# Expert weights in DRAM laid out partition by partition: one contiguous run a partition for each load

## The chip, the cores and the metric

The kernel runs on one core of one Trainium2 chip. The metric is the device time of one execution in microseconds. The work is split over the engines of the core: TensorE (PE, with its weight loads shown apart as PEld), VectorE (DVE), ScalarE (ACT), GpSimd (POOL), and SyncE (SP), which here issues nearly all transfers. Sixteen DMA engines move data between DRAM and the on-chip buffer of 128 partitions.

## The reference

The reference is a network of two blocks on 1024 tokens of width 1024, all in float32. The first block has dilated attention, a convolution and attention over a memory, then a convolutional feed-forward layer. The second has differential attention, a gated linear scan, neighbourhood attention, and then the mixture of experts that this change touches:

```python
def hier_moe(h, w_rg, b_rg, w_re, b_re, w_up, w_down):
    # each token picks a group, and 2 of the 8 experts in it (32 experts in all)
    # tokens are sorted by expert and padded to blocks, each block has one expert
    def expert_block(args):
        xb, e = args
        g, u = jnp.split(xb @ w_up[e], 2, axis=-1)
        return (jax.nn.silu(g) * u) @ w_down[e]
    y = lax.map(expert_block, (buf.reshape(n_blocks, MOE_BLOCK, D), blk_expert)).reshape(-1, D)
    y = y[dest] * gate.reshape(-1)[order][:, None].astype(h.dtype)
    return jax.ops.segment_sum(y, tok_sorted, num_segments=n_tok)
```

`w_up[e]` is 1024 x 1024 (4 MB in float32) and `w_down[e]` is 512 x 1024 (2 MB).

## The kernel before, in words

The program is one sequence of phases. The first block and the mixers of the second take about the first 2250 us. A routing phase then picks the experts and lists the tokens of each block, the phase `experts` computes the blocks, and `combine` gathers the results, normalises and stores them.

In `experts` a block is up to 96 tokens of one expert. The number of blocks depends on the routing; here 32 are worked on, in pairs: blocks 0 and 1 (with parts of the work on block 2) ahead of a loop, then a loop over pairs, then the tail of the last block. Each buffer is there twice, and `u` (0 or 1) is its half. The engines run the same loop beside each other and meet by semaphores. For block `(i, u)` the work is:

- GpSimd gathers the 96 token rows of 4 KB each into `xb` by an indirect transfer (line 3173), as soon as TensorE has turned the rows that were there before.
- TensorE turns the rows (`turn`, line 3205), and ScalarE scales them into `xT` (line 3280).
- TensorE multiplies by the gate half and by the up half of `w_up[e]` (`product` with s = 0 and s = 1; its matmuls stand at lines 3194 and 3196, in a helper that all products share). The first half waits for `u_ready[u]`, the landing of the 4 MB.
- ScalarE applies silu to the gate half (line 3294), VectorE multiplies by the up half (3347), TensorE turns the result (3227), and VectorE copies it (3339).
- TensorE multiplies by `w_down[e]` (`down`, again lines 3194 and 3196, after the wait for `d_ready[u]`); VectorE scales the result by the gate into `y` (3353); ScalarE issues three transfers to `y_dram` (3299 and 3301): 96 partitions of two runs of 1.5 KB, and twice 32 partitions of three runs of 512 bytes.

TensorE's order in the loop is: gate half of (i, 0), turn of the hidden values of the block before, turn of the rows of (i, 1), up half of (i, 0), `down` of (i-1, 1), gate half of (i, 1), turns, up half of (i, 1), `down` of (i, 0). So each block is followed over: a product, the two turns, a product, a `down`.

The weights are loaded by SyncE. `load_up` (line 2320) loads the 4 MB of an expert into `wu[:, u]`, shown in the profile as `big<-in_w_eup`. It waits for `up_done`, that is for the up half of the block two before, which frees the buffer. `load_down` (line 3150) loads 2 MB into `wd[:, u]` (`ex_wd<-in_w_edown`), and waits for the `down` of two blocks before. SyncE issues them in the fixed order up (i, 0), down (i-1, 1), up (i, 1), down (i, 0). The loads of blocks 0 and 1 are issued by the routing phase, the second once the rows of block 0 have landed. The expert's number is read into a register from the routing result, so the DRAM address is dynamic; its shape is not.

In DRAM the weights lie as in the input: expert, then row, then column. Partition p of the buffer holds the rows p, 128 + p, 256 + p and so on. Each is a run of 4 KB, and two runs of one partition lie 512 KB apart.

Of the kernel before, what the change touches and what calls it, by code (L numbers as in the profile page):

```python
# [16 lines left out]
P = 128  # L17
# [1333 lines left out]
def mid(nc, din, vecs, cst, h, hidden, po, V, w_down, down_ready, x_back, h_dram, h_back):  # L1351
# [13 lines left out]
    with Phase(nc, tag) as ph:  # L1365
# [72 lines left out]
        with nc.Block() as block:  # L1438
            @block.sync
            def _(sp):  # L1440
                def load_up(i):
                    if i == 1:

                        sp.wait_ge(sum_added, KD)
                    if i >= 2:

                        sp.wait_ge(hid_done, i - 1)
                    sp.dma_start(up[:, i % 2], din["w_up"][i]).then_inc(up_ready[i % 2], 16)

                load_up(0)  # L1450
                for j in range(4, n_po):
                    sp.wait_ge(po_done, 7 * (j // 2 - 1))
                    sp.dma_start(wp[:, j % 4], din["w_out"][j].rearrange("p (k n) -> p k n", k=KD)).then_inc(wp_ready[j % 4], 16)
                for k in range(KD):
                    sp.wait_ge(dve_kept, k + 1)
                    sp.dma_start(h_dram[:, k, :], h[:, k, :]).then_inc(h_stored, 16)
                for i in range(1, n_up):
                    load_up(i)

                sp.wait_ge(done, product_done(n_up - 1, 2))  # L1460
                sp.dma_start(w_down, din["w_down"][0]).then_inc(down_ready, 16)
                sp.wait_ge(done, product_done(n_up - 1, 6))
                sp.dma_start(h[:], h_dram).then_inc(h_back, 16)
# [849 lines left out]
def expert_of(eng, r, block):  # L2313

    at_block = bass.ds(block, 1) if not isinstance(block, int) else slice(block, block + 1)
    return eng.value_load(r["block"][0:1, at_block], min_val=0, max_val=E_ - 1)


def load_up(sp, din, e, wu, u, u_ready):
    sp.dma_start(wu[:, u], din["w_eup"][bass.ds(e, 1)].rearrange("a (k p) n -> p (a k) n", p=P)).then_inc(u_ready[u], 16)  # L2320


GLA_HALVES = (64, 32, 16, 8, 4, 2, 1)
# [438 lines left out]
def route(nc, tag, cst, vecs, din, h, mixed, wb, big, V, mod, a2, r, h2_dram, wu, u_ready, xb, x_ready):  # L2762
# [13 lines left out]
    with Phase(nc, tag) as ph:  # L2776
# [46 lines left out]
        with nc.Block() as block:  # L2823
            @block.sync
            def _(sp):
                sp.dma_start(wr[:], din["w_route"]).then_inc(route_in, 16)
                sp.dma_start(b_row[:], din["b_route"].partition_broadcast(P)).then_inc(route_in, 16)
                sp.dma_start(r["final"], din["final_row"].partition_broadcast(P)).then_inc(final_in, 16)
                for t in range(TT):
                    sp.wait_ge(evicted, t + 1)  # L2830
                    sp.dma_start(h2_dram[t * P:(t + 1) * P, :], rows[:, t % NR, :]).then_inc(row_stored[t % NR], 16)
                sp.wait_ge(first_ready, 1)
                load_up(sp, din, sp.value_load(r["first"][0:1, 0:1], min_val=0, max_val=E_ - 1), wu, 0, u_ready)
                sp.wait_ge(block_kept, 1)
                second = expert_of(sp, r, 1)
                sp.wait_ge(x_ready[0], 16)
                load_up(sp, din, second, wu, 1, u_ready)
                for u in range(NR):
                    sp.wait_ge(row_stored[u], 16 * len(range(u, TT, NR)))
                sp.wait_ge(final_in, 16)  # L2840
# [262 lines left out]
def experts(nc, tag, cst, din, r, ids, h2_dram, y_dram, y_filled, wu, u_ready, xb, x_ready, y, hid, a2, shift):  # L3103
# [8 lines left out]
    with Phase(nc, tag) as ph:  # L3112
        ph.sems += u_ready + x_ready
        wd = ph.sb("wd", [P, 2, KH, D])
# [8 lines left out]
        d_ready = [ph.sem("d_ready0"), ph.sem("d_ready1")]  # L3123
# [7 lines left out]
        def used(eng):  # L3131

            return eng.value_load(r["count"][0:1, 0:1], min_val=1, max_val=NB)

        with nc.Block() as block:
            @block.sync
            def _(sp):
                nb = used(sp)

                def load_gate_up(i, u):  # L3140
                    e = expert_of(sp, r, i * 2 + u)

                    sp.wait_ge(up_done, i * 2 + (u + 1))
                    load_up(sp, din, e, wu, u, u_ready)

                def load_down(i, u, block):
                    e = expert_of(sp, r, block)

                    sp.wait_ge(y_done, i * 2 + (u + 1))
                    sp.dma_start(wd[:, u], din["w_edown"][bass.ds(e, 1)].rearrange(  # L3150
                        "a (k p) n -> p (a k) n", p=P)).then_inc(d_ready[u], 16)

                load_down(0, 0, 0)
                with sp.Fori(1, NB // 2) as i:
                    with sp.If(i * 2 < nb):
                        load_gate_up(i, 0)
                        load_down(i - 1, 1, i * 2 - 1)
                        load_gate_up(i, 1)
                        load_down(i, 0, i * 2)
                pairs = sp.value_load(r["count"][0:1, 1:2], min_val=1, max_val=NB // 2)  # L3160
                load_down(pairs - 1, 1, pairs * 2 - 1)
# [474 lines left out]
def lay_out(x):  # L3636
# [29 lines left out]
    taps = np.concatenate([x["ffn_dw_w"][0], x["ffn_dw_b"]], axis=0).reshape(4, 2, KF, P).transpose(2, 3, 1, 0)  # L3666
    d["w_up"] = np.concatenate([up, taps.reshape(KF, P, 8)], axis=2)
    more(x, d, v, tables, col, wtiles, wrows)
    d["vec"] = np.concatenate([v[name] for name, _ in VECS], axis=1)
    return {k: np.ascontiguousarray(a) for k, a in d.items()}  # L3670


def more(x, d, v, tables, col, wtiles, wrows):

    w = x["w_in_2"][0]
    at_ = dict(zip(("qa", "ka", "va", "qb", "kb", "vb", "rb", "gb", "qn", "kn", "vn"),
                   np.split(w, np.cumsum((512, 512, 512, 128, 128, 256, 256, 32, 256, 256)), axis=1)))
    pad = np.zeros((D, 96), w.dtype)
    d["w_in2"] = wtiles(np.concatenate([at_["ka"], at_["kn"], at_["kb"], at_["gb"], pad, at_["qa"], at_["qn"],
                                        at_["qb"], at_["rb"]], axis=1))  # L3680
    d["w_v2"] = wrows(np.concatenate([at_["va"], at_["vn"], at_["vb"]], axis=1))
    d["w_mod"] = x["w_mod_2"][0].T.reshape(6 * KD, P, D)
    w2 = x["w_out_2"][0].reshape(KD, P, KD, P).transpose(2, 1, 0, 3)
    d["w_out2a"] = w2[:, :, [0, 1, 2, 3, 6, 7], :].reshape(KD, P, 6 * P)
    d["w_out2b"] = w2[:, :, 4:6, :].transpose(1, 0, 2, 3).reshape(P, KD, 2 * P)
    d["ctx"] = x["ctx_2"][0].T.reshape(KD, P, NCTX).transpose(1, 0, 2)
    dec = np.zeros((32, 2, P), w.dtype)
    for i in range(2):
        dec[16 * i:16 * i + 16, i] = x["gla_w_decay_2"][0, i]
    d["w_dec"] = np.concatenate([dec] * 4, axis=0)  # L3690
    i, j = np.arange(P)[:, None], np.arange(P)[None, :]
    d["gla_masks"] = np.stack([((i // (2 * m_) == j // (2 * m_)) & (i // m_ != j // m_)).astype(np.uint8) for m_ in GLA_HALVES],
                              axis=1)
    d["cos2"], d["sin2"] = tables["cos2"], tables["sin2"]

    p, y = np.arange(P)[:, None], np.arange(3 * P)[None, :]
    near = np.full((4, TT, P, 3 * P), NEG, w.dtype)
    for t in range(TT):
        row, c = 8 * (t // 4) + p // 16, 16 * (t % 4) + p % 16
        key_row, key_col = 4 * (t // 4) + y // 32, (0, 8, 24, 32)[t % 4] + y % 32  # L3700
        row0, col0 = np.clip(row - 4, 0, 8), np.clip(c - 8, 0, 48)
        seen = (key_row >= row0) & (key_row < row0 + 8) & (key_col >= col0) & (key_col < col0 + 16)
        dr, dc = np.where(seen, key_row - row + 7, 0), np.where(seen, key_col - c + 15, 0)
        for i in range(4):
            near[i, t][seen] = x["na_rel_bias_2"][0, i][dr, dc][seen]
    d["near"] = near.reshape(2, 2, TT, P, 3 * P).transpose(0, 2, 3, 1, 4).reshape(2 * TT, P, 6 * P)
    d["w_route"] = wrows(np.concatenate([x["w_router_group_2"][0], x["w_router_expert_2"][0]], axis=1))
    d["w_eup"], d["w_edown"] = x["w_expert_up_2"][0], x["w_expert_down_2"][0]
    lam = np.zeros((P, 4), w.dtype)
    lam[0:64] = x["diff_lambda_2"][0].T  # L3710
    d["final_row"] = x["final_g_2"]
    d["c"] = np.concatenate([x["c_2"][0], x["c_ctx_2"]])
    v.update({"g1": col(x["norm1_g_2"][0]),
              "g2": col(x["norm2_g_2"][0]), "b_mod": col(x["b_mod_2"][0]), "lam": lam,
              "sub_g": np.stack([x["diff_sub_g_2"][0]] * 4, axis=1),
              "gla_g": np.stack([np.tile(x["gla_norm_g_2"][0], 2)] * 2, axis=1),
              "b_dec": x["gla_b_decay_2"][0].T})
    d["b_route"] = np.concatenate([x["b_router_group_2"][0], x["b_router_expert_2"][0]])
# [15 lines left out]
```

## Time and profile before

| what | us |
|---|---|
| median of three runs | 2964.41 |
| lowest and highest of the runs | 2962.72, 2964.82 |
| span of the profiled execution | 2963.1 |
| TensorE busy in the span | 2816.7 |
| PE matmuls at lines 3194 and 3196 on the up weights, busy | 344.4 and 348.6 |
| DMA of 409.91 MB, mean over the span | 138 GB/s |

The span goes from the first to the last instruction of the profiled execution; the median of the runs is 1.3 us above it. The page lists groups of instructions by line, engine and operation. Some of them run at once, so their busy times overlap. What a stage is bound by is therefore read from starts, gaps and waits more than from the sum of busy times. In the page's strip of 40 slices the DMA engines are 9 tenths busy in slices 33 to 39, where the experts are, at 400 GB/s, and PE is 9 tenths busy there too.

### The profile page before, as it was taken

The page shows a single profiled execution, that of the slowest core. Times are in us where ns is not written, and L with a number is a line of the kernel's source. Part 1 is how long each engine was busy: PE and PEld are TensorE (multiplying, and loading weights), DVE is VectorE, ACT ScalarE, POOL GpSimd, SP SyncE. Part 2 cuts the span into 40 slices and gives each one's busy share as a digit, 9 for nine tenths or more (in the row PEclk, how much of TensorE's full clock was granted, in tenths as well). Part 3 has the DMA queues.
Part 4 walks back from the last instruction along what each step waited for, and adds up shares of the span by engine and source line. Part 5 has one row for each costly group of instructions (what it writes and reads, how often), then busy time and mean ns, then how long its engine had stood idle before and what let it go on. Part 6 is the DMA issues. An engine that isn't in the chain of part 4 may idle for free. (4 is left out here: it accounts for less than half of the span.)

```text
span 2963.1 us, 44007 instructions
## 1 busy us (share of the span) xinstructions
PE 2816.7 (95%) x18379; PEld 1669.6 (56%) x18379; DVE 1414.2 (48%) x1968; ACT 808.4 (27%) x1503; POOL 63.2 (2%) x90
## 2 busy tenths in 40 slices
PE   8999999999999998999999998999999799999995
PEld 4434564444444443444454444656555699999994
DVE  6843676566666664444553005867674211111113
ACT  2101572111111114333200105757332211112111
POOL 0000000000000000000000000000000000000002
PEclk9999999999999999999999999999999899999997
DMA  3112761211111115332232000004200999999995
GB/s 137 54 43 39 196 208 58 86 43 43 43 43 43 43 55 230 130 131 112 81 83 67 29 0 11 1 1 116 94 12 10 351 400 399 402 402 403 402 353 181
DMA packets 118420, 409.91 MB, mean 138 GB/s; under 512 B 9536, under 2 KB 28480, under 8 KB 113568
## 3 DMA queue, kind: packets, MB, share of 16 engines
q1 hardware_dynamic: 98480, 374.35, 34.7%
q0 software_dynamic: 6000, 21.37, 2.2%
q10 hardware_dynamic: 13824, 12.59, 1.2%
q8 instruction: 80, 1.31, 0.2%
q14 instruction: 36, 0.29, 0.0%
HBM read 367.38 MB, written 51.38 MB: 141 GB/s over the span
## 5 line engine op out<-in xcount | busy, mean ns | idle before, releaser
L3194 PE MATMUL ex_up_ps<-big,ex_xT 128*32 128x384 f32 x3072 | 344.4, 489 | 13.7 <-DMA big<-in_w_eup 6.7
L3196 PE MATMUL ex_up_ps<-big,ex_xT 128*32 128x128 f32 x3072 | 348.6, 274 | 0.0
L3196 PEld LDWEIGHTS ex_up_ps<-big,ex_xT 128*32 128x32 f32 x3072 | 331.3, 110 | 0.4
L1927 PE MATMUL dn_acc<-big,V 128*128 128x512 f32 x704 | 304.8, 595 | 1.6 <-PEq L43 1.6
L1927 PEld LDWEIGHTS dn_acc<-big,V 128*128 128x128 f32 x704 | 134.4, 191 | 170.3 <-issue 170.3
L1542 PE MATMUL fm_ring<-h,V 128*128 128x512 f32 x504 | 219.7, 592 | 0.0
L937 PE MATMUL f_acc<-h,f_w 128*128 128x512 f32 x416 | 182.4, 598 | 0.0
L3196 PE MATMUL ex_y_ps<-ex_wd,ex_hT 128*32 128x128 f32 x1536 | 175.7, 275 | 0.0
L293 DVE TENSOR_SCALAR_CACHE_REDUCE h<-ad_s_ps 128x1280 f32<-128x1280 f32 x64 | 92.9, 1489 | 172.6 <-PE ad_s_ps L202 172.6
L3194 PE MATMUL ex_y_ps<-ex_wd,ex_hT 128*32 128x384 f32 x1536 | 173.6, 492 | 0.8 <-DVE ex_hT L3339 0.8
L3196 PEld LDWEIGHTS ex_y_ps<-ex_wd,ex_hT 128*32 128x32 f32 x1536 | 169.4, 111 | 0.7
L1542 PEld LDWEIGHTS fm_ring<-h,V 128*128 128x128 f32 x504 | 95.8, 190 | 120.5 <-issue 120.5
L1583 ACT ACTIVATE po_w<-po_w,fm_up 128x1024 f32<-128x1024 f32 x44 | 54.2, 1233 | 343.1 <-DVE po_w L1698 341.1
L3194 PEld LDWEIGHTS ex_up_ps<-big,ex_xT 128*32 128x32 f32 x3072 | 127.5, 110 | 24.9 <-issue 21.2
L937 PEld LDWEIGHTS f_acc<-h,f_w 128*128 128x128 f32 x416 | 79.2, 191 | 100.6 <-issue 100.6
L3294 ACT ACTIVATE big<-ex_up_ps 128x384 f32<-128x384 f32 x32 | 15.7, 490 | 419.9 <-PE ex_up_ps L3196 419.9
L3347 DVE TENSOR_TENSOR big<-big,ex_up_ps 128x384 f32<-128x384 f32 x32 | 17.7, 554 | 195.2 <-PE ex_up_ps L3196 195.2
L2028 ACT ACTIVATE dn_prod<-dn_prod 128x1024 f32<-128x1024 f32 x96 | 100.6, 1049 | 19.6 <-DVE dn_prod L2134 19.3
L3353 DVE TENSOR_TENSOR big<-ex_y_ps,big 128x768 f32<-128x768 f32 x32 | 30.7, 958 | 155.4 <-PE ex_y_ps L3196 155.4
L3280 ACT ACTIVATE ex_xT<-ex_x_ps,mod,a 128x96 f32<-128x96 f32 x264 | 88.6, 441 | 44.7 <-PE ex_x_ps L3205 44.7
L3339 DVE COPY ex_hT<-ex_h_ps 128x384 f32<-128x384 f32 x32 | 17.8, 558 | 172.7 <-PE ex_h_ps L3227 172.7
L202 PE MATMUL ad_s_ps<-big 64*128 64x256 f32 (+1 forms) x448 | 79.3, 491 | 13.4 <-DVE h L293 11.3
(550 smaller groups left out, 4507.5 us busy)
## 6 DMA issues: line engine op xcount, KB each, us to landing
big<-in_w_eup SPq DMA_DIRECT2D x32, 4096.0 KB
ex_wd<-in_w_edown SPq DMA_DIRECT2D x32, 2048.0 KB, 22.8
fm_up<-in_w_up SPq DMA_DIRECT2D x22, 1028.0 KB, 4.9
y_dram<-in_cos SPq DMA_DIRECT2D x1, 21504.0 KB, 73.1
dn_tail<-in_w_mod SPq DMA_DIRECT2D x32, 512.0 KB, 6.9
V<-in_w_down SPq DMA_DIRECT2D x8, 1408.0 KB, 6.8
y_dram<-big ACTq DMA_DIRECT2D x32, 288.0 KB
dn_tail<-in_w_in SPq DMA_DIRECT2D x17, 512.0 KB, 3.5
```

The source lines that it names most:

```text
L202: mm = nc.tensor.matmul(s_ps[:, i % SB, u, o:o + w], q[r, m, t * P:(t + 1) * P], keys[s][0][r, m, a:a + w], start=True, stop=True)
L293: ins = V.tensor_scalar(p, s, 1.0 if diff is None else -SCALE, 3.0e38, ALU.mult, ALU.min, accum_out=low)
L937: mm = nc.tensor.matmul(acc[:, j % 2, a:a + width], w[:, j % R, k, :], src[:, k, a:a + width], start=(k == 0), stop=(k == KD - 1))
L1542: mm = nc.tensor.matmul(bank(i, j), wj[:, k, :], bj[:, k, :], start=(k == 0), stop=(k == 3))
L1583: nc.scalar.activation(y[:, s, :], raw[:, s, :], ACT.Identity, bias=taps[:, 4 * s + 3:4 * s + 4], scale=taps[:, 4 * s + 1:4 * s + 2]).then ...
L1927: mm = nc.tensor.matmul(o[:, x * BANK:(x + 1) * BANK], wd[j % 2][:, k * P:(k + 1) * P], hidden[:, k, x * BANK:(x + 1) * BANK], start=(k == ...
L2028: last = nc.scalar.activation(prod[:, m % 2, a, :], prod[:, m % 2, a, :], ACT.Copy, accum_out=mod[:, m:m + 1, a])
L3194: nc.tensor.matmul(o[32 * g:32 * g + 32, 0:W], rows(g), w[:, 0:W], start=first, stop=last)
L3196: mm = nc.tensor.matmul(o[BR:P, g * P:(g + 1) * P], rows(g), w[:, W:BANK], start=first and g == 0, stop=last and g == GR - 1)
L3280: ins = nc.scalar.activation(xT[:, u, k, :], x_ps[:, k, 0:BR], ACT.Identity, bias=shift[:, k:k + 1], scale=a2[:, k:k + 1])
L3339: nc.vector.tensor_copy(hT[:], h_ps[:]).then_inc(hT_ready, 1)
L3353: nc.vector.tensor_tensor(y[:, u], y_ps[:, :, 0:W], r["gate5"], ALU.mult).then_inc(y_kept, 1)
```

## The change

The host lays both weight tensors out so that what one partition of the buffer holds is contiguous in DRAM: for each expert, partition by partition, 32 KB for the up weights (8 rows of 4 KB) and 16 KB for the down weights (4 rows of 4 KB). The two loads name the DRAM side and the buffer side as 128 runs of 8192 or 4096 elements. The same bytes reach the same places in the buffer. The number of transfers, their order, their queue and all semaphores stay as they are, and so do the instructions of the other engines. The layout is made ahead of the launch, with the other inputs' layouts.

```diff
 def load_up(sp, din, e, wu, u, u_ready):
-    sp.dma_start(wu[:, u], din["w_eup"][bass.ds(e, 1)].rearrange("a (k p) n -> p (a k) n", p=P)).then_inc(u_ready[u], 16)
+    sp.dma_start(wu[:, u].rearrange("p k n -> p (k n)"), din["w_eup"][bass.ds(e, 1)].rearrange("a p n -> (a p) n")).then_inc(u_ready[u], 16)
...
                     sp.wait_ge(y_done, i * 2 + (u + 1))
-                    sp.dma_start(wd[:, u], din["w_edown"][bass.ds(e, 1)].rearrange(
-                        "a (k p) n -> p (a k) n", p=P)).then_inc(d_ready[u], 16)
+                    sp.dma_start(wd[:, u].rearrange("p k n -> p (k n)"), din["w_edown"][bass.ds(e, 1)].rearrange(
+                        "a p n -> (a p) n")).then_inc(d_ready[u], 16)
...
-    d["w_eup"], d["w_edown"] = x["w_expert_up_2"][0], x["w_expert_down_2"][0]
+    def by_partition(w):
+        return w.reshape(w.shape[0], -1, P, w.shape[2]).transpose(0, 2, 1, 3).reshape(w.shape[0], P, -1)
+
+    d["w_eup"], d["w_edown"] = by_partition(x["w_expert_up_2"][0]), by_partition(x["w_expert_down_2"][0])
```

## Rows read from the trace of the kernel before

**Rows 1.** Engines by stretch: start and end, length, busy us (count), clock, DMA share, GB/s.

```profile
2400.00:2800.00 400.00, 389.96 (x6784) 377.25 (x6778) 46.65 (x68) 73.01 (x207) 25.77 (x46) 1.00 1.03 401
2311.00:2319.00 8.00, 5.55 (x35) 5.12 (x35) 6.07 (x19) 0.00 (x0) 0.00 (x0) 0.58 1.02 419
1112.40:1118.40 6.00, 0.00 (x0) 0.00 (x0) 3.62 (x4) 2.19 (x2) 0.00 (x0) 0.53 1.01 437
```

**Rows 2.** Waits of TensorE, 2320 to 2910 us: us in total, times, longest.

```profile
PE ex_up_ps L3194 <- DMA big<-in_w_eup: 6.7, 14, 0.8
PE ex_up_ps L3194 <- issue: 6.2, 14, 1.6
PE ex_x_ps L3205 <- DMA xb<-h_dram,ex_idx: 1.3, 1, 1.3
```

**Rows 3.** Timeline of PE, from a `down` to the next block's gate half, three times.

```profile
2519.09 0.50 PE L3194 MATMUL ex_y_ps<-ex_wd,ex_hT 128*32 128x384 f32 x3
...
2520.07 0.52 PE L3194 MATMUL ex_up_ps<-big,ex_xT 128*32 128x384 f32 x3 [0.32 <-issue]
...
2871.08 0.50 PE L3194 MATMUL ex_y_ps<-ex_wd,ex_hT 128*32 128x384 f32 x3
...
2871.41 0.50 PE L3194 MATMUL ex_up_ps<-big,ex_xT 128*32 128x384 f32 x3
...
2359.11 0.50 PE L3194 MATMUL ex_y_ps<-ex_wd,ex_hT 128*32 128x384 f32 x3
...
2359.91 0.52 PE L3194 MATMUL ex_up_ps<-big,ex_xT 128*32 128x384 f32 x3
```

**Rows 4.** The loop's gathers into `xb`: duration ns min/median/max, first and last start.

```profile
L3173 POOL DMA_INDIRECT xb<-h_dram,ex_idx x32: 938/938/943, 2327.6 to 2844.7; - x32
```

**Rows 5.** Timeline of ScalarE, silu of blocks 1, 15, 30, 31: start, length, idle before.

```profile
2348.06 0.49 ACT L3294 ACTIVATE big<-ex_up_ps 128x384 f32<-128x384 f32 x1 [7.93 <-PE ex_up_ps L3196]
...
2596.06 0.49 ACT L3294 ACTIVATE big<-ex_up_ps 128x384 f32<-128x384 f32 x1 [13.64 <-PE ex_up_ps L3196]
...
2860.03 0.49 ACT L3294 ACTIVATE big<-ex_up_ps 128x384 f32<-128x384 f32 x1 [13.66 <-PE ex_up_ps L3196]
2877.03 0.49 ACT L3294 ACTIVATE big<-ex_up_ps 128x384 f32<-128x384 f32 x1 [13.10 <-PE ex_up_ps L3196]
```

**Rows 6.** DMA in 2311 to 2319 us, then in 1112.4 to 1118.4 us: packets, by size.

```profile
DMA packets 818, 3.35 MB, mean 419 GB/s; under 512 B 0, under 2 KB 0, under 8 KB 817
...
DMA packets 80, 2.62 MB, mean 437 GB/s; under 512 B 0, under 2 KB 0, under 8 KB 0
```

**Rows 7.** Timeline of SyncE: the up loads of blocks 1 and 2.

```profile
2323.52 0.39 SPq L2320 DMA_DIRECT2D big<-in_w_eup  x1
...
2342.95 0.38 SPq L2320 DMA_DIRECT2D big<-in_w_eup  x1
```

**Rows 8.** DMA queues in 2419 to 2423 us: packets, MB, share of 16 engines.

```profile
q1 hardware_dynamic: 337, 1.38, 83.5%
q10 hardware_dynamic: 335, 0.28, 20.7%
```

**Rows 9.** DMA queues in 2331 to 2340 us, where two gathers stand beside weight loads.

```profile
q1 hardware_dynamic: 533, 2.13, 70.9%
q0 software_dynamic: 224, 0.79, 31.1%
```

**Rows 10.** Timeline of PE: it turns the rows of block 1.

```profile
2336.53 0.88 PE L3205 MATMUL ex_x_ps<-pack,xb 96*128 96x96 f32 x8 [1.28 <-DMA xb<-h_dram,ex_idx]
```

**Rows 11.** First packets: weight load in 2324 to 2325 us, gather in 2331 to 2332 us.

```profile
q1 hardware_dynamic: 7, 0.03, 25.1%
...
q0 software_dynamic: 7, 0.03, 7.0%
```

**Rows 12.** Timeline of GpSimd: one block's index copy, ahead of its gather.

```profile
2526.84 0.18 POOL L3169 COPY ex_idx<-ids 128x1 int32 x1 [15.61 <-PE ex_x_ps L3205]
```

**Rows 13.** DMA queues in 2400 to 2800 us (q10: `y` stores, q0: gathers).

```profile
q1 hardware_dynamic: 35484, 142.42, 89.4%
q0 software_dynamic: 2576, 9.05, 7.0%
q10 hardware_dynamic: 9936, 9.05, 6.5%
```

**Rows 14.** VectorE's step that waits for the `y` buffer, from the page.

```profile
L3353 DVE TENSOR_TENSOR big<-ex_y_ps,big 128x768 f32<-128x768 f32 x32 | 30.7, 958 | 155.4 <-PE ex_y_ps L3196 155.4
```

## The prediction, made before the changed kernel was run

> **What bounds the kernel now.** The change touches only the expert stage, so I read the stretches first, then TensorE's waits, then the timelines around one wait. In the 400 us from 2400 to 2800, TensorE's matmuls are busy 389.96 us and the DMA engines have a share of 1.03 at 401 GB/s [rows 1]. Both look full, so the waits have to say which of them sets the pace. TensorE's largest repeated waits in the stage stand before the first product of a block, 14 put down to the landing of the up weights and 14 to "issue", 12.9 us together [rows 2]. The reader is to see in the timeline that both kinds are one: at 2519.09 the last step of a `down` starts and the next block's product follows 0.98 us later, at 2871.08 it follows 0.33 us later [rows 3]. The second is block 31, the last. Its load differs from the others in one thing: no gather competes with it any more, the last one being issued at 2844.7 [rows 4]. So the full-length gap is a wait for weights, and DMA sets the pace.
>
> The silu starts give the price. From block 1 (2348.06) to block 31 (2877.03) there are 30 periods in 528.97 us, 17.63 us each; the last period, without the wait, is 2877.03 - 2860.03 = 17.00 us; block 15 stands where an even pace puts it [rows 5]. That is what TensorE needs for a block when weights are there.
>
> Is DMA itself used fully? A block moves 6.29 MB of weights, 0.39 MB of gathered rows and 0.39 MB of results, 7.08 MB; at 401 GB/s that is 17.6 us, the period. The queue is never empty.
>
> **The change part by part.** No instruction is moved, added or removed, on no engine and in no queue: one transfer stands for one transfer. What changes is the size of the packets.
>
> 1. Rate. Alone on the engines, the up load in rows of 4 KB makes 419 GB/s, in 2311 to 2319 us. The trace also has a load whose DRAM side has just the new form, 128 runs of 32 KB one behind the other: `h` back from `h_dram`, in 1112.4 to 1118.4 us. There 80 packets carry 2.62 MB, so a packet is a whole run of 32 KB, and the rate is 437 GB/s [rows 1, 6]. An engine needs 4096 x 16 / 419 GB/s = 0.1565 us for a packet of 4 KB and 6.0 / 5 = 1.2 us for one of 32 KB. A straight line through both (0.007 us for a packet and 0.0373 us a KB) puts 16 KB at 0.604 us. Each of the 16 engines serves 8 partitions. Before: 96 packets of 4 KB, 15.02 us a block. After: 8 of 1.2 and 8 of 0.604, 14.43 us. Saved: 0.59 us of DMA time a block. Bounds: 0 (419 GB/s stays, the mixed traffic hides the gain) and 0.65 (437 for both sizes).
>
> The Trainium skill's page "DMA: Bandwidth & Descriptors", section "Why small descriptors are slow (HBM only)", counts about three cycles for each packet beside one cycle for each 32 bytes. By that, 4 KB costs 131 cycles where 128 carry data, and the saving would be some 2% of 15.02, or 0.3 us, an estimate from that page. The measured pair of rates gives twice that, and I go by the rates.
>
> 2. The new period. The DMA side alone would give 17.63 - 0.59 = 17.04 us. TensorE gives 17.00 for the odd blocks. The even blocks begin a pass of the loop, which may cost TensorE something of its own. The first pass has a gap of 0.80 us against 0.33, where the load was early: it was issued 17 us before, at 2342.95, at a time when the queue had run empty, and takes some 10 us by its rate [rows 3, 7]; that is 0.47 us more, with the entry of the loop in it, and 0 is the other bound. Taking the middle, an even block is 17.24 and the mean 17.12. The two sides now meet within 0.1 us, and where two limits meet neither is reached quite, so I take 17.15. What is late next is thus TensorE itself. From 30 x (17.63 - 17.15) comes 14.4 us saved. Bounds: 30 x (17.63 - 17.00) = 18.9 and 0.
>
> 3. The start. Queues share an engine packet by packet. In 2419 to 2423 us, q1 (weights) moved 337 packets and q10 (results) 335, though those of q1 are far larger [rows 8]. The gathers do the same beside the loads [rows 9]. So a small packet waits for one packet of the weights, now 1.2 or 0.6 us instead of 0.16. The one gather on whose landing TensorE waits is that of block 1: its turn starts at 2336.53, after a wait of 1.28 us [rows 10]. The gather has 6 rows and one closing packet on each engine (224 packets for two gathers, over 16 engines, is 7), and its packets begin to move at about 2331.9. By then the second up load, running since about 2324.9 [rows 11] with 1.2 us a packet, has about three packets left, and the down load's 16 KB packets follow. Seven turns are then 3 x 1.2 + 4 x 0.6 + 7 x 0.20 (31.1% of 9 us and 16 engines over 224 packets [rows 9]) = 7.4 us, an end at 2339.3 instead of 2336.3, just before the turn. TensorE has nothing else to do there, and everything behind it moves: plus 3.0 us. Bounds: 0 (the engine splits long packets) and 7 x 1.4 less the 4.4 of now, 5.4 us. Later gathers are issued as soon as the rows two blocks before are turned [rows 12], so they have two periods, some 34 us, and a landing that is 10 us later costs nothing. If that cover were gone, each would cost its lateness.
>
> 4. The stores of `y`. Each block sends 27 packets an engine through q10 (9936 packets in 23 blocks, over 16 engines) [rows 13], against 16 data and 2 closing packets of the new weight loads. The store of a block, now through in a few us (335 of its 432 packets in 4 us [rows 8]), will stretch over more than one block. The step that needs its buffer comes two blocks later and today never waits for it: all its idle time is put down to PE [rows 14]. TensorE needs that step only before the next `down`, some 11 us later. So there is room of about 44 us, and I price it at 0. Without that cover it is the rival below.
>
> Sum, against the profiled execution: 2963.1 - 14.4 + 3.0 = 2951.7 us of span, and 1.3 us more for the median of the runs: 2953.0. The likeliest case's own range is 2945.5 (18.9 saved, nothing lost at the start) to 2959 (a period of 17.35, which saves 8.4, and 3.0 lost).
>
> **The rivals.**
>
> *A, hardly any change.* The gain of the rate shows up only where the loads are alone. Beside gathers the whole traffic falls, for all 16 engines, to some 2.92 MB in 9 us, 325 GB/s, from 419 [rows 9], so the mix has costs that no packet size of q1 touches, and the even blocks could cost TensorE 0.47 us more in any pass. With half the saving, 0.3 us a block, and the 3.0 us at the start it is 30 x 0.3 - 3.0 = 6, so 2958.4; with a tenth of a us a block, 2964.4. I set it to 2961. The gap that vanishes in the last block speaks against a TensorE that is the bound, the 32 KB row against no gain in rate.
>
> *B, slower: the stores starve.* The Trainium skill, same page, section "Queues, rings and completion order", says that each engine takes turns between its queue rows at packet boundaries; the trace agrees (337 to 335). Worked out from the rows: while weights are queued, q10 gets one packet for each of q1, 18 in a block, and needs 27. The nine left over pass only when q1 is empty. They need 9 x 0.042 = 0.4 us (6.5% of 400 us and 16 engines over 9936 packets [rows 13]). My sum leaves q1 empty for 17.15 - 14.43 less 1.22 for the gather (7.0% of 400 us over 23 blocks) and 0.75 for the 18 packets, so 0.75 us. If that falls short, 9 packets a block pile up, and after 4 or 5 blocks the room of 44 us is gone. Then VectorE waits for the `y` buffer, TensorE for VectorE, SyncE's next load is issued late, and q1 stays empty until the new load's first packets move, 1.4 us after its issue (2323.52, first packets in 2324 to 2325 [rows 7, 11]). A block is then about 17.04 + 1.4 = 18.4 us, for some 24 blocks: 24 x 0.8 + 3.0 = 22, so 2986. It decides from the point where q1 is empty for less than 0.4 us a block. Against it: a stop of TensorE itself empties q1, so the fault heals itself, and at once.
>
> *C, the change doesn't do what it says.* The DRAM side could still be cut into 4 KB packets. Then nothing happens: 2964.4. The 80 packets of 32 KB speak against it; they have the same form but a fixed address.
>
> **How the numbers follow.** This kernel's measurement can tell about 0.2% from no change, 5.9 us, so faster is below 2958.5 and slower above 2970.3. The forecast has 0.64 and lies in "faster". Rival A has 0.18, of which 0.04 falls in "faster"; C has 0.04, in "same". B has 0.14, of which 0.12 is "slower"; its mild end, a short-lived backlog, is "same". So faster 0.68, same 0.20, slower 0.12. The range from 2945 to 2966 leaves out most of B and little of the rest.
>
> **What would show it.** Right: packets of q1 in 2400 to 2800 fall from 35484 to about a fifth; q1 alone shows about 437 GB/s; the period of silu starts is 17.1 to 17.2 and the waits of TensorE before the first product shrink to the loop's own; the DMA share in the stage falls under 1; TensorE's wait for block 1's rows grows from 1.3 to about 4 us. Wrong: VectorE's step at line 3353 waiting for a DMA (B); a period at 17.6 with fewer packets (A: the mix decides); packets still at 4 KB (C); the first turn not later (step 3: long packets are split).

## The result: slower by 0.3%, and the profile after

| | median us | lowest to highest | runs |
|---|---|---|---|
| before | 2964.61 | 2962.52 to 2967.94 | 6 |
| changed | 2971.78 | 2968.64 to 2978.68 | 6 |

The ratio is 1.0032, with a 95% interval from 1.0022 to 1.0042. The changed kernel is about 7 us slower, where I had forecast 11 us faster. Its runs also lie 10 us apart, against 5 us before. The profiled execution is the fastest of them (2968.64 us, span 2966.8), so what follows explains the 3.7 us by which its span exceeds that of before; the other five runs left no trace.

The table of DMA queues of the changed kernel in 2400 to 2800 us answers to [rows 13]:

```profile
q1 hardware_dynamic: 6582, 144.02, 86.8%
q10 hardware_dynamic: 9972, 9.10, 6.9%
q0 software_dynamic: 2483, 8.66, 6.2%
```

The change does what it says: the weight queue q1 moves its 144 MB in 6582 packets, where 142 MB took 35484. The page's list of DMA issues (count, KB each, us from issue to landing) shows how long each kind now takes:

```profile
big<-in_w_eup SPq DMA_DIRECT2D x32, 4096.0 KB, 14.6
ex_wd<-in_w_edown SPq DMA_DIRECT2D x32, 2048.0 KB, 15.8
y_dram<-big ACTq DMA_DIRECT2D x32, 288.0 KB, 13.9
```

The down loads land after 15.8 us where the list of before had 22.8. TensorE's waits in 2320 to 2915 us answer to [rows 2]:

```profile
PE ex_y_ps L3194 <- DVE ex_hT L3339: 14.1, 4, 7.3
...
PE ex_x_ps L3205 <- DMA xb<-h_dram,ex_idx: 6.0, 1, 6.0
PE ex_up_ps L3194 <- ACT ex_xT L3280: 0.6, 1, 0.6
```

The 28 waits for weights before the first product of a block are gone; the one of 0.6 us for `xT` was there before too. Two others have grown: 6.0 us at the start for the rows of block 1 (1.28 before), and 14.1 us in four waits for VectorE (one of 0.8 us before). The timeline of ScalarE shows where the time is. These are the silu of blocks 3 to 8 (start, length, idle before), to be read against [rows 5]:

```profile
2388.06 0.49 ACT L3294 ACTIVATE big<-ex_up_ps 128x384 f32<-128x384 f32 x1 [13.09 <-PE ex_up_ps L3196]
...
2405.06 0.49 ACT L3294 ACTIVATE big<-ex_up_ps 128x384 f32<-128x384 f32 x1 [13.08 <-PE ex_up_ps L3196]
...
2426.99 0.49 ACT L3294 ACTIVATE big<-ex_up_ps 128x384 f32<-128x384 f32 x1 [18.02 <-issue]
...
2454.58 0.49 ACT L3294 ACTIVATE big<-ex_up_ps 128x384 f32<-128x384 f32 x1 [24.51 <-issue]
...
2473.99 0.49 ACT L3294 ACTIVATE big<-ex_up_ps 128x384 f32<-128x384 f32 x1 [16.34 <-issue]
...
2483.05 0.49 ACT L3294 ACTIVATE big<-ex_up_ps 128x384 f32<-128x384 f32 x1 [5.98 <-PE ex_up_ps L3196]
```

The period is 17.00 us where it runs free. From 2405.06 to 2483.05 four periods take 77.99 us instead of 68.0. A second such group, from 2704.00 to 2779.59, takes 75.59. TensorE's idle time is the larger part of these 17.6 us, and a lower clock comes on top, as the stretches of the two groups show:

```profile
2405.00:2483.00 78.00, 70.33 (x1198) 68.16 (x1198) 8.00 (x12) 12.40 (x36) 4.49 (x8) 0.96 0.98 393
...
2704.00:2780.00 76.00, 70.36 (x1201) 68.33 (x1202) 8.09 (x12) 12.81 (x37) 4.49 (x8) 0.96 0.98 389
```

TensorE is idle for 7.7 and 5.6 us there, 13.3 in all, and its granted clock is 0.96, where the 217 us between the groups have 1.00. Right behind the longest wait, in 2454 to 2458 us, it is 0.65. In each group, VectorE waits for the landing of the result stores, as its timeline shows:

```profile
2423.98 0.96 DVE L3353 TENSOR_TENSOR big<-ex_y_ps,big 128x768 f32<-128x768 f32 x1 [11.76 <-DMA y_dram<-big]
...
2451.16 0.96 DVE L3353 TENSOR_TENSOR big<-ex_y_ps,big 128x768 f32<-128x768 f32 x1 [22.03 <-DMA y_dram<-big]
...
2470.84 0.96 DVE L3353 TENSOR_TENSOR big<-ex_y_ps,big 128x768 f32<-128x768 f32 x1 [15.02 <-DMA y_dram<-big]
```

Before, this step never waited for a DMA [rows 14]. The DMA queues say why. First 2441 to 2444 us, in a group of stops, then 2468 to 2471 us, at its end (packets, MB, share of 16 engines):

```profile
q1 hardware_dynamic: 36, 1.18, 91.0%
q10 hardware_dynamic: 36, 0.01, 1.6%
```

```profile
q1 hardware_dynamic: 41, 0.41, 32.1%
q0 software_dynamic: 72, 0.28, 28.3%
q10 hardware_dynamic: 322, 0.24, 23.8%
```

As in [rows 8], the queues take turns packet by packet, 36 to 36, but a turn of q1 now lasts 1.2 us: in 3 us the stores move 0.01 MB. Only when q1 runs dry do they get through, 322 packets in 3 us.

How the stores fall behind shows in the blocks ahead of the first group. First the period from 2371.06 to 2388.06, then one between the groups, from 2534.04 to 2551.03:

```profile
q1 hardware_dynamic: 286, 6.23, 88.6%
...
q10 hardware_dynamic: 285, 0.33, 5.5%
```

```profile
q1 hardware_dynamic: 285, 6.19, 86.4%
q10 hardware_dynamic: 435, 0.40, 7.4%
```

A block makes 432 packets of stores. In the first stretch, and in the period behind it (283 and 283), they get one turn for each weight packet and some 150 are left over. Between the groups they nearly keep pace: 5124 packets in the 12 periods from 2500.04 to 2704.00, where 5184 are due. The room shrinks from block to block: 8 us into the period from 2500.04, 236 packets of stores and 21 of weights start in 2 us, and at the same place in the last period ahead of the second group (2695 to 2697 us) it is 97 and 33. Why it shrinks stays open.

Where the profile's 3.7 us come from, counted from silu to silu: block 1 to block 31 takes 527.84 us instead of 528.97. That is 19.0 us saved by the period, less 10.0 and 7.6 for the two groups and 0.3 for the first pass. The start, from the silu of block 0 to that of block 1, takes 17.89 us instead of 11.45, so 6.4 us are lost. The stage begins 0.8 us sooner and its tail is 0.9 us shorter, which the change does not explain. -1.1 + 6.4 - 0.8 - 0.9 is 3.6.

### The profile page after: what moved, and what is told of

The parts are those of the page before. It is cut to its first block and busy times, and to the rows that moved or that the text cites. A ratio compares the mean times of both kernels' runs of the same rounds, so it can differ in the third digit from the quotient of the medians.

```text
span 2966.8 us, 44007 instructions
## 1 busy us (share of the span) xinstructions
PE 2817.8 (95%) x18379; PEld 1674.7 (56%) x18379; DVE 1413.9 (48%) x1968; ACT 808.5 (27%) x1503; POOL 63.2 (2%) x90
## 5 line engine op out<-in xcount | busy, mean ns | idle before, releaser
L3194 PE MATMUL ex_y_ps<-ex_wd,ex_hT 128*32 128x384 f32 x1536 | 176.4, 498 | 14.1 <-DVE ex_hT L3339 14.1
L3347 DVE TENSOR_TENSOR big<-big,ex_up_ps 128x384 f32<-128x384 f32 x32 | 17.7, 554 | 187.4 <-PE ex_up_ps L3196 177.3
L1683 DVE TENSOR_TENSOR V<-fm_ring,V 128x512 f32<-128x512 f32 x63 | 43.6, 692 | 100.3 <-PE fm_ring L1542 99.6
## 6 DMA issues: line engine op xcount, KB each, us to landing
big<-in_w_eup SPq DMA_DIRECT2D x32, 4096.0 KB, 14.6
ex_wd<-in_w_edown SPq DMA_DIRECT2D x32, 2048.0 KB, 15.8
```

Of the source, the lines that this page charges most:

```text
L1683: return V_.tensor_tensor(out, a, b, op)
L3194: nc.tensor.matmul(o[32 * g:32 * g + 32, 0:W], rows(g), w[:, 0:W], start=first, stop=last)
```

## The experiments

Two theories could explain the stops. Theory T (turns): packets of different queues take turns, and the weights now have too few packets, so the stores get too few turns. Rival L (layout): the new place of the bytes in DRAM is at fault. Later came a question on the gathers, theories M and G. In e1, e3, e4, e11, e12 and e13 the new layout is padded in DRAM, 256 bytes behind each run, so that a run cannot be longer than I want it; the 4096 elements shown here are 1024 or 2048 in others:

```diff
-    sp.dma_start(wu[:, u].rearrange("p k n -> p (k n)"), din["w_eup"][bass.ds(e, 1)].rearrange("a p n -> (a p) n")).then_inc(u_ready[u], 16)
+    runs = din["w_eup"][bass.ds(e, 1)].rearrange("a p (c n) -> (a p) c n", n=4096+64)[:, :, 0:4096]
+    sp.dma_start(wu[:, u].rearrange("p k n -> p (k n)").rearrange("p (c n) -> p c n", n=4096), runs).then_inc(u_ready[u], 16)
...
+        return np.pad(w, ((0, 0), (0, 0), (0, 0), (0, 64))).reshape(w.shape[0], P, -1)
```

| kernel | packets up, down | median us | ratio to before (95%) |
|---|---|---|---|
| e1_4k | 4, 4 KB | 2962.87 | 1.000 (0.999 to 1.001) |
| e2_few_stores | 32, 16 | 2950.75 | 0.9962 (0.9948 to 0.9976) |
| e3_16k_8k | 16, 8 | 2970.61 | 1.0028 (1.0018 to 1.0038) |
| e4_8k | 8, 8 | 2958.44 | 0.9991 (0.9979 to 1.0002) |
| e5_up_only | 32, 4 | 2975.22 | 1.0046 (1.0029 to 1.0063) |
| e6_start_rows | 32, 16 | 2971.50 | 1.0029 (1.0017 to 1.0042) |
| e7_small_gather | 32, 16 | 2951.48 | 0.9962 (0.9950 to 0.9975) |
| e8_sync_stores | 32, 16 | 2983.63 | 1.0069 (1.0052 to 1.0085) |
| e9_gather128 | 32, 16 | 2956.14 | 0.9986 (0.9977 to 0.9996) |
| e10_before_gather128 | 4, 4 | 2951.55 | 0.9962 (0.9951 to 0.9974) |
| e11_8k_start | 8, 8 | 2959.50 | 0.9995 (0.9983 to 1.0007) |
| e12_16k_8k_g128 | 16, 8 | 2947.57 | 0.9955 (0.9938 to 0.9973) |
| e13_8k_start_g128 | 8, 8 | 2946.48 | 0.9944 (0.9928 to 0.9961) |

The kernel before had medians of 2962.19, 2962.09, 2961.65 and 2964.09 us beside the four sets of runs (e1 to e4, e5 to e8, e9 to e11, e12 and e13). Each kernel was traced in one of its runs, which need not be like its median: the trace of e2 is of its slowest run (2957.30), those of e6 and e7 of their fastest (2960.97 and 2946.27). e2 leaves part of the result unstored, and e7 most of the rows ungathered.

**The new place, the old packets.** 

> The new layout partition by partition, but with 256 bytes of padding behind each 4 KB in DRAM, so that a packet is again 4 KB. Theory T (turns): the loss comes from too few, too long weight packets, against which the 27 packets of a block's result stores get one turn each. With 96 data packets a block no store falls behind: VectorE never waits for a store, the period is that of before, about 17.6 us, TensorE waits for block 1's rows about 1.3 us, and the time is that of before, 2962 to 2966 us. Rival L (layout): the loss comes from where the bytes lie in DRAM (16 engines reading 256 KB apart). Then the stops of 75 us groups stay and the time is 2968 or more.

2962.87 us, the time of before. The period (17.61 us), the wait for block 1's rows (0.8 us) and the queues' numbers are near those of before. Rival L falls: where the bytes lie does nothing here, for good or ill, as far as this layout, with its 256 bytes of padding, stands for the changed kernel's.

**Fewer stores against the same packets.** The edit leaves out the two small stores:

```diff
-    PARTS = 3
+    PARTS = 1
...
-                    for c in range(2):
-                        act.dma_start(dst[:, c, W:BANK].rearrange("(g p) n -> p g n", g=GR), ...
```

> The changed kernel with 32 and 16 KB packets, but the two small stores of each block (32 partitions, three runs of 512 bytes) are left out, so that part of the result is not written. A block then has 13 store packets an engine instead of 27, against 18 of the weights. Theory T: no pile-up, VectorE's step for y never waits for a DMA, all periods are 17.0 us, about 17.6 us less than the changed kernel in its two groups of stops; the later start stays. Expected 2950 to 2953 us. Rival L, or one in which long packets stall the engines by themselves: the stops stay, 2968 us or more. The bytes left out are small (0.1 MB of 7.1 MB a block, some 0.3 us), too little to explain more than the pace.

2950.75 us. No stop; the periods are 17.0 us up to block 10 and 17.13 us on average behind it, while the trace lists a single wait for weights, of 0.3 us. Theory T stands.

**More turns.** 

> The new layout with padding so that a partition's up weights come in two packets of 16 KB and its down weights in two of 8 KB. A block has 32 data packets and 2 closing ones, more than the 27 of the stores. Theory T: no stop, period 17.0 us, the gather of block 1 waits for packets of half the length, so TensorE's wait for it lies between 1.3 and 6.0 us, about 3. Expected 2946 to 2951 us. Rival L: as the changed kernel, 2968 or more.

2970.61 us, 20 us above what I expected. No stop, as theory T has it, but the period is not 17.0 and not even 17.6. The timeline of ScalarE shows 17.6 and 18.0 in turn, with TensorE waiting for weights before each block:

```profile
2495.37 0.49 ACT L3296 ACTIVATE big<-ex_up_ps 128x384 f32<-128x384 f32 x1 [14.15 <-PE ex_up_ps L3198]
...
2513.01 0.49 ACT L3296 ACTIVATE big<-ex_up_ps 128x384 f32<-128x384 f32 x1 [13.73 <-PE ex_up_ps L3198]
...
2531.01 0.49 ACT L3296 ACTIVATE big<-ex_up_ps 128x384 f32<-128x384 f32 x1 [14.10 <-PE ex_up_ps L3198]
```

So something beside the stores makes DMA slower when packets are longer, although q1 alone is faster.

> The new layout in packets of 8 KB for both weights: 48 data packets a block. Theory T: no stop; DMA needs 48 times 0.306 us, 14.7 us, for the weights of a block, still 0.3 us less than with 4 KB; with the other queues' 2.4 to 2.6 us that is 17.1 to 17.3, so some of the waits for weights come back: period 17.0 to 17.2 us. The first gather is nearly as early as before. Expected 2945 to 2951 us. Rival L: 2968 or more.

2958.44 us, a period of 17.5 and a start 2.6 us late. The interval holds 1, so a gain is not shown. The trace has the same unknown cost, smaller.

**One half of the change.** The down load is put back to its old layout and rows.

> Only the up half of the change: 32 KB packets for the up weights, 4 KB rows for the down weights as before. A block has 8 + 32 data packets and 2 closing ones, more than the 27 of the stores. Theory T: no stop in any run, so the times lie close together; the down load's short packets also let the gather through. But the packets of 8 and 16 KB runs showed that the mix beside gathers is slower than the weights alone, so the period is expected at 17.5 us, not 17.0, and the start is late by some 4 to 6 us. 2962 to 2968 us. If long packets alone are at fault, without the count of turns: stops as in the changed kernel, 2968 and more.

2975.22 us, within 3.5 us of each other: no stop, as theory T has it, but a period of 17.7 to 18.7 from block 4 to block 30, the slowest kernel of all that leave the stores in ScalarE's queue. The mechanism of stops is absent and the kernel is slower still. So long packets have a second cost, which here comes in place of the stops; the changed kernel does not show it as a longer period, being at 17.00 us between its groups.

**The start.**

```diff
-                load_up(sp, din, second, wu, 1, u_ready)
+                load_up_rows(sp, din, second, wu, 1, u_ready)     # the second copy, in 4 KB rows
```

(and the first `load_down` alike.) 

> The changed kernel, except that the up weights of block 1 and the down weights of block 0 come from a second copy in the old layout, in 4 KB rows. These are the loads beside which the gather of block 1 runs. Theory T: TensorE's wait for those rows falls from 6.0 back to about 1.3 us, and the silu of block 1 comes about 6 us earlier; the stops of the steady part stay. 2962 to 2972 us, 5 to 6 us under the changed kernel. Rival: the late start has another cause (the addresses, or instruction fetches); then the wait stays at 6 us.

2971.50 us with runs from 2960.97 to 2977.25: the median is that of the changed kernel (2971.78), and a gain of 6 us is not shown in it. The trace shows the start by itself: TensorE's wait is 1.1 us and the silu of block 1 follows that of block 0 after 11.25 us instead of 17.89. Its two groups of stops cost 13.6 and 7.2 us, more than in the changed kernel's trace. The late start is settled by that trace; its price in the median is not.

**The gathers.**

```diff
-                    pool.indirect_dma_start(xb[0:BR, u, :], None, h2_dram, ...ap=idx[0:BR, u:u + 1]
+                    pool.indirect_dma_start(xb[0:n, u, :], None, h2_dram, ...ap=idx[0:n, u:u + 1]      # n = 16
```

> The changed kernel, but from block 3 on only 16 of the 96 rows are gathered (2 packets an engine instead of 7), so the blocks are computed on rows left there from before. It asks whether it is the gather's cost beside long packets that eats the time in which the stores could catch up. Then the stores keep pace, the stops vanish, every period is 17.0 us, and the time is 2950 to 2953 us. If the stops come from the count of store packets alone, whatever the gather does: stops as before, 2965 and more.

2951.48 us: no stop in the trace, every period 17.0 from block 3 on. With most of the gather's bytes gone the stores catch up with their 27 packets against 18. So the stops need both, few turns and the gather.

**The stores in line instead of in turn.** SyncE issues them, behind the down load that is due at the same event.

```diff
+                        load_down(j, 1, j * 2 + 1)
+                        store_y(j * 2 - 1, 1, j * 2 + 1)        # the three transfers, now in SyncE's queue
...
-                        store_y(i - 1, 1)                       # ScalarE's
```

> The changed kernel with its 32 and 16 KB packets, but SyncE issues the stores of y, in the queue of the weights, each behind the down load that is issued at the same event. They then take no turns against the weights, but stand in line with them, at most some 15 us, of the 44 us that there are. Theory T: no stop, period 17.0 us, the late start stays: 2949 to 2953 us. Rival: the stores' small packets cost the same wherever they are issued, or hold up the weight loads in line behind them; then TensorE waits for weights, period 17.4 us or more, 2962 or more.

2983.63 us, the slowest: theory T's number missed by 30 us, and the time lies on the rival's side. No stop, as T says, but a period of 18.2 to 18.4 us for most blocks in which TensorE waits for weights, as the rival says. With the stores in line only the gather still takes turns with the long packets, and the mean traffic in 2400 to 2800 us is 389 GB/s, against 401 before.

The changed kernel has the same packets and the same gathers and yet holds 17.00 us between its stops. The traces show the difference. First one gather of the changed kernel, 2540 to 2544 us, then one of this kernel, 2540 to 2549 us:

```profile
q1 hardware_dynamic: 59, 0.93, 61.7%
q0 software_dynamic: 111, 0.39, 30.0%
```

```profile
q1 hardware_dynamic: 140, 2.54, 82.2%
q0 software_dynamic: 112, 0.39, 13.7%
```

Between the changed kernel's stops the weights have landed before the next are due, 14.6 us behind the issue of an up load against 24.4 here. So q1 runs nearly dry once a block (a share of 24.3% in 2542 to 2543 us), and gather and stores pass then. In this kernel q1 is behind all the time, the gather's packets take turns with long packets for twice as long, and the mean traffic in these 9 us is 326 GB/s. That a kernel which is late with its weights has dear gathers and so stays late is how I read it.

**Why a gather costs so much.** In ten microseconds with one gather in them, the kernel before shows this. The first row is GB/s in slices of 0.25 us, from 2530 to 2540 us:

```profile
GB/s 410 430 426 410 426 426 410 442 410 426 360 279 344 311 279 279 295 311 295 393 426 410 442 377 442 410 426 410 393 442 410 410 410 377 426 426 377 442 393 426
DMA packets 1017, 3.91 MB, mean 391 GB/s; under 512 B 54, under 2 KB 64, under 8 KB 1017
```

For about 2.2 us the traffic of all queues falls from 415 to some 300 GB/s. The next two kernels gather 128 rows into all 128 partitions, where 96 are used:

```diff
-                    pool.indirect_dma_start(xb[0:BR, u, :], None, h2_dram, ...ap=idx[0:BR, u:u + 1]
+                    pool.indirect_dma_start(xb[:, u, :], None, h2_dram, ...ap=idx[:, u:u + 1]
```

> The changed kernel with 128 rows gathered for each block from block 1 on instead of 96 (the 32 more are a copy of row 0 that nobody uses). A gather of 96 rows gives each of the 16 engines 6 partitions, the weight load gives each 8. Theory M (mismatch): while a gather runs, engines write into partitions that others are filling, and the whole traffic falls from about 420 to about 345 GB/s; with 128 rows each engine stays with its own 8 partitions, the fall is gone or halved, the stores keep pace and there are fewer stops: 2952 to 2962 us. Rival G: a gather's packets are slow in themselves; then 8 instead of 6 of them a block make it worse: more stops, 2972 us or more.

2956.14 us: one group of stops instead of two, of 6.3 us (74.28 us for four periods), and 0.14% faster than before.

> The kernel before, with its 4 KB rows, and 128 rows gathered for each block. DMA sets its pace, so what a gather costs is seen at once in the period of 17.6 us. Theory M: the fall beside a gather from 415 to 345 GB/s goes, which saves about 0.5 us, against 0.13 MB more, 0.3 us: period 17.4 us, 2955 to 2960 us. Rival G: 8/6 of the gather's cost: period 17.9 to 18.1 us, 2971 to 2978 us.

2951.55 us, 10 us faster than before with a third more rows to gather, and better than theory M's own number: the period is 17.2 us, not 17.4. The row of ten microseconds with one gather in them, 2525 to 2535 us:

```profile
GB/s 436 373 473 354 481 377 410 475 360 475 377 426 475 360 459 377 426 492 360 443 377 426 492 377 426 377 442 475 377 426 426 410 475 377 410 475 344 475 377 426
DMA packets 1148, 4.20 MB, mean 420 GB/s; under 512 B 58, under 2 KB 132, under 8 KB 1148
```

The dip is gone. 128 rows against 96 is the edit, and it takes the dip away. Why is not shown. My guess is theory M: a gather of 96 rows has 112 packets, 7 an engine with the closing one, so 6 partitions an engine where the weights have 8, and an engine would write into partitions that another is filling. No run shows which engine fills which partition. That the 32 rows more all come from one address was not varied by itself.

**Together.** 

> The packets of 8 KB, and the up weights of block 1 and the down weights of block 0 from a copy in 4 KB rows, as the best of both: TensorE's wait for the rows of block 1 falls from about 4 us to 1.3, the period stays at 17.5 us. 2.5 us under the kernel with 8 KB alone: 2954 to 2958 us. If the start gave nothing, 2957 to 2960.

2959.50 us, above the 2954 to 2958 expected, against 2958.44 for 8 KB alone, which comes from another set of runs: not told apart, though the trace shows block 1 on time (11.62 us behind block 0). The 2.5 us are not shown.

> Packets of 16 and 8 KB, which with gathers of 96 rows ran at a period of 17.8 us without a stop, now with gathers of 128 rows. Theory T + M: 34 weight packets a block are more than the 27 of the stores, so no stop; and the gather no longer pulls the traffic down, so DMA needs 14.6 us for weights, 1.2 for the gather and 1.1 for the stores, 16.9 in all: period 17.0 us from block 3 on, and about 4 us lost at the start. 2946 to 2950 us. Rival: the slow period of 17.8 comes from the length of the packets itself; then it stays above 17.4 us, 2960 or more.

2947.57 us. The two kernels with packets of 16 and 8 KB in ten microseconds with one gather each, that of 96 rows first (2535 to 2545 us) and that of 128 rows below (2526 to 2536 us):

```profile
DMA packets 723, 3.73 MB, mean 373 GB/s; under 512 B 76, under 2 KB 333, under 8 KB 429
```

```profile
DMA packets 852, 4.23 MB, mean 423 GB/s; under 512 B 90, under 2 KB 387, under 8 KB 515
```

With 4 KB packets such a stretch had 391 and 420. So longer packets make the 96-row gather dearer; with 128 rows they cost nothing in such a stretch. The period went from 17.8 to 17.0 us, and the 400 us from 2400 hold not one wait of TensorE.

> Packets of 8 KB, gathers of 128 rows, and the two loads beside the first gather from a copy in 4 KB rows: the version to which the runs point. Period 17.0 to 17.1 us and no loss at the start: 4 to 6 us under the kernel before with gathers of 128 rows, 2944 to 2948 us. If the packet size gave nothing once the gather is cured: 2951 us.

2946.48 us, the fastest: 0.56% under the kernel before (0.39 to 0.72), period 17.0 to 17.05 us, no late start. Engines by stretch, as in [rows 1]:

```profile
2400.00:2800.00 400.00, 400.00 (x7044) 392.37 (x7047) 48.15 (x70) 75.89 (x215) 27.48 (x48) 1.00 1.02 424
```

TensorE is busy in all 400 us. The ratio of e10, which has the 128 rows and 4 KB packets, is 0.9962. That leaves 0.2% for the packets, and the intervals overlap: a gain by longer packets is not shown in the time, though the period is 17.0 us against e10's 17.2.

## Why the prediction was wrong

The step that failed is step 4: the stores of `y` were priced at 0 and cost 17.6 us in the profiled run, because the time of q1 beside other traffic (step 1) was too low. Step 3, the start, was right in kind and too small. The steps in turn:

**The bound now: right.** DMA set the pace and TensorE needed 17.00 us. e7 and e12 run at exactly that, and so does the changed kernel between its stops. The extra of 0.47 us that I gave the even blocks doesn't exist in the steady loop: even and odd periods are both 17.00. The term was too high by 0.12 us a block, so the full 0.63 us a block were there to be won, 18.9 us.

**Step 1, the rate: right alone, wrong in the mix.** The changed kernel's own up load, with one other packet in 2311 to 2317 us, answers to [rows 6]:

```profile
DMA packets 80, 2.60 MB, mean 433 GB/s; under 512 B 0, under 2 KB 0, under 8 KB 0
```

433 GB/s against the 437 assumed and the 419 of 4 KB. The step failed where it took the rate of q1 alone for its rate in the mix. It gave q1 14.43 us of a block; in the changed kernel's periods ahead of the stops q1 takes 88.6% and 89.1% of 17.00 us, 15.1 us. And rival A read [rows 9], 325 GB/s beside gathers, as a cost "that no packet size of q1 touches". It depends on packet size: a stretch of ten microseconds with one gather has 391 GB/s at 4 KB and 373 at 16 and 8 KB. e3, e5 and e8 show the price, periods of 17.6 to 18.7 us where my sum gave 17.0; e12 takes it away by the gather alone. That it is the number of turns times their length (7 turns of up to 1.2 us) is how I read it. From issue to landing a gather takes 8.9 us in the changed kernel, 10.3 in e3, 11.1 in e5 and 12.5 in e8, which fits; only e7, with 2 packets an engine instead of 7, varied the number of turns, and it has 5.9. The estimate of 2% that the prediction works out from the Trainium skill, page "DMA: Bandwidth & Descriptors", section "Why small descriptors are slow (HBM only)", and the 3 to 4% measured alone decide nothing here. The upper bound of 0.65 us in that step comes out at 0.62 when worked again; nothing rests on it.

**Step 3, the start: the mechanism right, the size wrong.** Forecast 3.0 us (bounds 0 and 5.4), measured 6.4. The wait rose from 1.28 to 6.0 us, so 4.7 us come from the longer turns, which e6 confirms. The other 1.7 us are nearly all the clock. TensorE had stood still for 6 us; in 2341 to 2347 us of the changed kernel its granted clock is 0.74, where the same product before had 1.00 in 2337 to 2342:

```profile
2341.00:2347.00 6.00, 6.00 (x83) 5.47 (x85) 0.00 (x0) 2.69 (x8) 1.12 (x2) 0.74 0.71 216
```

0.74 is a mix of the two levels, 1.2 and 2.4 GHz, and 6 us at 0.74 are 1.6 us less than at full clock. A wait of TensorE of this length cost more than the wait itself.

**Step 4, the stores: priced at 0, and the step on which the sign turned.** It cost 17.6 us in the profiled run (20.8 in the trace of e6). Rival B described it: turns one to one, 18 against 27, VectorE's step for `y` waiting for a store, from the fourth or fifth block. It got 0.14 because I reckoned q1 empty for 0.75 us a block: 17.15 less 14.43 for q1, 1.22 for the gather and 0.75 for the stores. The gather's share did not grow (5.9% and 6.6% of the periods from 2371.06 and 2388.06, so 1.0 and 1.1 us). It is the 14.43 that was wrong, and 15.1 leaves nothing: 285 packets of stores pass beside 286 of the weights, one to one, with no spare time. e7 gives the time back by a shorter gather, and the stops vanish. e2 takes the packets away, and they vanish too. B's price was off too: TensorE does not stop by 1.4 us a block but in groups that cost 10.0 and 7.6 us here, after which 13 blocks run free, since a dry q1 lets a whole backlog through (787 packets in the period from 2483.05) and then runs nearly dry once a block. And the room was not 44 us: ScalarE issues the stores ahead of the next silu in its own order, so a `y` step that waits holds the silu back at once, and the 11 us that I added for TensorE's next `down` do not exist. The silu rows of the groups, with 16 to 25 us of idle time put down to "issue", are that wait.

**What was luck.** Without the stops the profiled run would be near 2951 us, and e2 and e7, which have none, are at 2950.75 and 2951.48, close to the 2953.0 of the sum. That agreement is in part luck: the period gave 19.0 us where the sum had 14.4, and the start cost 6.4 where it had 3.0.

Rival A (no gain) and C (no effect) were not the case, though A's "the mix decides" was the nearer sentence.

## What to carry to other kernels

A DMA packet is also the length of a turn. Before making one queue's packets longer, count the packets of each other queue in the same period. While the long queue is not empty, another queue gets one packet through for each of its packets; whatever it needs beyond that must wait until the long queue runs dry. Here that was 27 against 18. And a transfer that something waits for is late by up to its own packets an engine times the long packet's time: 7 packets beside 32 KB ones took some 8 us in e8. Where a stage moves at DMA's pace, look at the traffic in slices beside each kind of transfer: here the dip beside one small gather was worth more (10 us, by gathering more rows) than all the packet sizes (at most 5 us more, and not told apart).

## What the runs showed of the hardware that I had not expected

- A gather of 96 rows of 4 KB into 96 partitions pulls the traffic of all queues from about 415 to 300 GB/s for some 2 us beside 4 KB packets; one of 128 rows into 128 partitions leaves it at 420.
- Queues alternate one to one even where a packet of one is 32 KB and of the other 512 bytes or less (36 and 36 in 3 us). Long packets are not split: the 36 of q1 carry 1.18 MB.
- The rows of a partition one behind the other (with 256 bytes between them) or 512 KB apart: no difference as long as packets are 4 KB (2962.87 and 2962.19 us).
- The same gathers and packets can run at two paces: 17.00 us a block where q1 runs nearly dry once a block, 18.2 to 18.4 where it never does (changed kernel between its stops, and e8).
- Alone, packets of 4 KB make 419 GB/s and of 32 KB 433 to 437.
